# Modulation rows turned four at a time, and heads' products in two split passes, in a two-layer diffusion trunk on one core

## The reference

```
mod = silu(cond) @ w_ada + b_ada                 # (group, 6 * 1024)
h = rms_norm(x, norm1_g) * (1 + sc1) + sh1
z = h @ w_in                                     # 3,360 columns for mixers, 4,096 gate logits
aq, ak = rms_norm(a_q per head of 64), rms_norm(a_k per head of 64)
cq, ck = rms_norm(c_q per head of 32), rms_norm(c_k per head of 32)
aq, ak, cq, ck = apply_rope(...)                 # latent tokens only: y = x*cos + rot(x)*sin
...                                              # attention A and C, gated recurrences B and D
x = x + g1 * (sum(sigmoid(logits) * branches) @ w_out)
x = x + g2 * conv_ffn(rms_norm(x)*(1+sc2)+sh2)
```

## Time and profile before

| | |
|---|---|
| median of 3 runs | 2597.76 us (2597.54 to 2599.13) |
| profiled execution, its own time | 2600.3 us |
| span of the profiled execution | 2598.5 us |
| granted clock of TensorE, mean | 0.976 of full |
| busy: PE, PE weight loads, DVE, ACT | 95%, 89%, 52%, 35% |
| moved by DMA | 228.54 MB, 88 GB/s |

### The profile page before, as it was taken

One profiled execution on the slowest core, in us unless ns is written; L12 is line 12 of the kernel. 1 busy time (PEld: TensorE's weight loads), 2 busy tenths in 40 slices (PEclk: granted clock), 3 DMA queues, 4 the chain that ended last, 5 costly groups with the idle time before them and its releaser, 6 DMA issues.

```text
span 2598.5 us, 50531 instructions
## 1 busy us (share of the span) xinstructions
PE 2471.3 (95%) x22106; PEld 2303.3 (89%) x22106; DVE 1343.4 (52%) x2075; ACT 919.6 (35%) x1290; POOL 2.2 (0%) x6
## 2 busy tenths in 40 slices
PE   5999899899999999999989998979999999999998
PEld 3889776788999899999989996768899989999998
DVE  4123366786755655454241325768775654555621
ACT  4244355322243533333232435542222543333410
POOL 0000000000000000000000000000000000000000
PEclk8999899899999999999999998989999999999999
DMA  8645111122235222213244331102222622222222
GB/s 252 198 156 165 31 43 37 44 55 59 63 126 160 65 69 77 81 50 98 77 143 138 110 95 41 47 26 53 52 63 79 206 65 66 81 70 71 68 70 71
DMA packets 323607, 228.54 MB, mean 88 GB/s; under 512 B 17952, under 2 KB 317024, under 8 KB 322656
## 3 DMA queue, kind: packets, MB, share of 16 engines
q1 hardware_dynamic: 317584, 211.32, 27.8%
q10 hardware_dynamic: 5840, 14.51, 1.7%
HBM read 215.44 MB, written 10.35 MB: 87 GB/s over the span
## 4 chain that ended last, share of the span: by engine, by line
PE 83%; DVE 10%; ACT 3%; issue 2%; DMA 1%; SPq 0%; DVEq 0%; ACTq 0%
PE PS L681 21%; PE PS L682 21%; PE PS L683 21%; PE PS L883 2%; DVE RING_split L1740 2%; PE PS L850 2%; PE PS L898 1%; PE PS L705 1%; PE PS L914 1%; PE PS L670 1%; PE PS L993 1%; DVE BIG L1914 1%; PE PS L793 1%; PE PS L852 1%; PE PS L794 1%
## 5 line engine op out<-in xcount | busy, mean ns | idle before, releaser
L681 PE MATMUL PS<-HH_split,WHI_split 128*128 128x320 f32 x3168 | 999.8, 316 | 21.4 <-DVE HL_split L1715 8.6
L683 PE MATMUL PS<-HH_split,RING_split 128*128 128x320 f32 x3136 | 973.6, 310 | 0.0
L682 PE MATMUL PS<-HL_split,WHI_split 128*128 128x320 f32 x2912 | 905.9, 311 | 0.0
L681 PEld LDWEIGHTS PS<-HH_split,WHI_split 128*128 128x128 f32 x3168 | 600.1, 189 | 36.0 <-issue 25.2
L683 PEld LDWEIGHTS PS<-HH_split,RING_split 128*128 128x128 f32 x3136 | 593.2, 189 | 0.0
L682 PEld LDWEIGHTS PS<-HL_split,WHI_split 128*128 128x128 f32 x2912 | 552.5, 190 | 1.9 <-issue 1.9
L1740 DVE TENSOR_TENSOR RING_split<-RING,WHI_split 128x1024 fp32r<-128x1024 f32 (+2 forms) x204 | 274.6, 1348 | 473.0 <-ACT WHI_split L1473 235.2
L682 PE MATMUL PS<-ZT_split,WHI_split 128*128 128x320 f32 x1216 | 377.1, 310 | 0.0
L682 PEld LDWEIGHTS PS<-ZT_split,WHI_split 128*128 128x128 f32 x1216 | 229.5, 189 | 0.0
L1747 DVE TENSOR_TENSOR RING_split<-RING,WHI_split 128x1024 fp32r<-128x1024 f32 x52 | 62.4, 1223 | 263.0 <-ACT WHI_split L1215 262.9
L1473 ACT ACTIVATE WHI_split<-RING 128x1024 fp32r<-128x1024 f32 x88 | 93.3, 1060 | 289.6 <-PE PS L683 289.6
(11 more groups left out here) (215 smaller groups left out, 3293.6 us busy)
## 6 DMA issues: line engine op xcount, KB each, us to landing
RING<-in_w_in SPq DMA_DIRECT2D x96, 512.0 KB, 4.0
RING<-in_w_up SPq DMA_DIRECT2D x88, 512.0 KB, 5.0
RING<-in_w_ada SPq DMA_DIRECT2D x80, 512.0 KB, 6.1
RING<-in_w_down SPq DMA_DIRECT2D x32, 384.0 KB, 3.6
RING<-in_w_in SPq DMA_DIRECT2D x40, 256.0 KB, 3.3
RING<-in_w_down SPq DMA_DIRECT2D x32, 320.0 KB, 4.0
RING<-in_w_out SPq DMA_DIRECT2D x16, 512.0 KB, 4.7
ZT<-in_w_ada SPq DMA_DIRECT2D x8, 1024.0 KB, 10.0
```

Of the source, the lines that this page charges most:

```text
L681: release(pe.matmul(out, w_hi, hi[:, a:b], start=begin, stop=False), fresh and a == 0)
L682: pe.matmul(out, w_hi, lo[:, a:b], start=False, stop=False)
L683: ins = pe.matmul(out, w_lo, hi[:, a:b], start=False, stop=end)
```

## The change

Four things are changed.

1. After the first 8 modulation chunks, chunks go in sets of four (ADA_SET). The condition columns stand in SC32 with zeros on both sides, and a window on it places the two result rows of chunk r of a set at rows 2r and 2r + 1; the other rows get zeros, so the four products add up in one PSUM tile. Only the fourth is copied out, and one turn with 8 columns of SEL gives the set. The 8 chunks for layer 1 come in plain order so that sets are contiguous.
2. The heads' mean squares and the rotations are made in the split type: ACT rounds the operand (HI), DVE subtracts (LO), and PE makes two passes, HI and LO, against constants that are exact in the split type (copied once at the start by DVE).
3. Orders of issue: in layer 0's first tiles turn 4 comes before the products, modulation 6 and 7 one k apart, ACT's row copies before `modulate_two`, and DVE's weight rests before `modulation_first(1)`. ACT reads decay 0 (`decay_in(0)`) after the first tile of the last chunk.
4. `unit_order` looks two chunks ahead only after the second tile of chunk 3.

```diff
-        jobs = [(l, s) for s in range(N_ADA1, N_ADA_Z)] + ([(l + 1, s) for s in ADA1] if l + 1 < DEPTH else [])
+        jobs = [(l, s) for s in range(N_ADA1, N_ADA_Z)] + ([(l + 1, s) for s in range(N_ADA1)] if l + 1 < DEPTH else [])
...
+ADA_SET = 4
+def ada_row(a):
+    return 0 if a < N_ADA1 else (a - N_ADA1) % ADA_SET
+def ada_turns(a):
+    return a + 1 if a < N_ADA1 else N_ADA1 + (a - N_ADA1) // ADA_SET + 1
...
-            while nxt < U_MIX and nxt <= done + LEAD and chunk[nxt] <= c + (2 if c + 1 == QK_AT else 1):
+            while nxt < U_MIX and nxt <= done + LEAD and chunk[nxt] <= c + (2 if c + 1 == QK_AT and n == 1 else 1):
...
                 def ada_turn(a):
-                    pe.wait_ge(row_kept, a + 1)
+                    n = 1 if a < N_ADA1 else ADA_SET
+                    pe.wait_ge(row_kept, ada_turns(a))
                     for h in range(2):
-                        at = ada_at(a) + 2 * h
-                        last = pe.matmul(ada_columns(a)[:, at:at + 2], ROW[a % 2][:, h * P:(h + 1) * P], SEL[:], start=True, stop=True)
+                        out = ada_columns(a)[:, ada_at(a - n + 1):ada_at(a - n + 1) + 4 * n].rearrange("p (s h c) -> p s h c", h=2, c=2)[:, :, h, :]
+                        last = pe.matmul(out, ROW[ada_turns(a) % 2][:, h * P:(h + 1) * P], SEL[:, 0:2 * n], start=True, stop=True)
...
-                    if l == 0 and k == 1:
-                        first_turn(4)
                     if l == 0 and k == 2:
                         ada(5)
                         first_turn(5)
-                    if l == 0 and k == 4:
+                    if l == 0 and k == 3:
                         ada(6)
                         first_turn(6)
+                    if l == 0 and k == 4:
                         ada(7)
                         first_turn(7)
...
-                    wide(pair(2), BLK64 if QK_TILES[i][2] == 64 else BLK32, SQ[i % 2], True, True).then_inc(qk_ms, 1)
+                    pe.wait_ge(consts_split, 1)
+                    blocks = BLK64_R if QK_TILES[i][2] == 64 else BLK32_R
+                    wide(pair(2), blocks, SQ_HI[i % 2], True, False)
+                    wide(pair(2), blocks, SQ_LO[i % 2], False, True).then_inc(qk_ms, 1)
...
-                    pe.wait_ge(qk_normed, l * NQK + (i + 1))
-                    if i:
-                        pe.wait_ge(qk_done, l * NQK + i)
-                    pe.matmul(pair(3)[:, 0:TS], ROTA if hd == 64 else ROTC, ZT[:, t, 0:TS], start=True, stop=True).then_inc(qk_rot, 1)
+                    pe.wait_ge(rot_lo, l * NQK + (i + 1))
+                    turn_by = ROTA_R if hd == 64 else ROTC_R
+                    pe.matmul(pair(3)[:, 0:TS], turn_by, ROT_HI, start=True, stop=False)
+                    pe.matmul(pair(3)[:, 0:TS], turn_by, ROT_LO, start=False, stop=True).then_inc(qk_rot, 1)
...
+                        if n == 0 and 0 <= c - QK_AT - 2 < NQK:
+                            head_round(c - QK_AT - 2)
+                        if c == NC_Z - 1 and n == 0:
+                            decay_in(0)
...
+            nv.tensor_copy(CONST_R[:, 2 * P:], CONST[:, 2 * P:]).then_inc(consts_split, 1)
```

More of the change, by code:

```diff
@@ L704, in ada @@
                     for k in range(KT):
-                        last = pe.matmul(ada_out(a)[32 * (k % 4):32 * (k % 4) + 32], SC32[:, k, :], raw(RING, i, 0, 256, 256, KT)[:, k, :],
-                                         start=k < 4, stop=k >= 4)
+                        last = pe.matmul(ada_out(a)[32 * (k % 4):32 * (k % 4) + 32], SC32[:, k, SC_AT - 2 * ada_row(a):SC_AT - 2 * ada_row(a) + 32],
+                                         raw(RING, i, 0, 256, 256, KT)[:, k, :], start=k < 4 and ada_row(a) == 0,
+                                         stop=k >= 4 and (a < N_ADA1 or ada_row(a) == ADA_SET - 1))
                         release(last, k == 0, inside)
@@ L752, in _ @@
                             first_turn(a - 1)
+                    first_turn(4)
                 def head_mean_square(i):
@@ L1081, in late_turn @@
                         at = 4 * n + 2 * h
-                        last = pe.matmul(LATE_COLUMNS[:, at:at + 2], ROW[n % 2][:, h * P:(h + 1) * P], SEL[:], start=True, stop=True)
+                        last = pe.matmul(LATE_COLUMNS[:, at:at + 2], ROW[n % 2][:, h * P:(h + 1) * P], SEL[:, 0:2], start=True, stop=True)
                     last.then_inc(late_turned, 1)
@@ L1318, in _ @@
                 log_and_exp()
[L1319 to L1324 removed]
+                decay_in(1)
                 act.wait_ge(al_lin, l * 2 + 2)
@@ L1792, in _ @@
                 for c in range(NC_Z):
-                    for g, kind, dst, j in Z_TILES[c]:
+                    for n, (g, kind, dst, j) in enumerate(Z_TILES[c]):
                         for u in UNITS_AT[U_Z[g]]:
```

93 lines of the change are left out of this document (61 added, 32 removed).

## The result

| kernel | median of its runs, us | ratio to the kernel before, with 95% interval |
|---|---|---|
| before, 4 runs | 2598.45 (2597.54 to 2604.91) | |
| the change, 4 runs | 2566.88 (2563.29 to 2568.43) | 0.9862 [0.9851, 0.9874] |
| the same change again, later, 4 runs | 2565.58 (2564.58 to 2567.84) | 0.9864 [0.9849, 0.9879] |

The change is faster by 1.4%, or 31.6 us between the medians; 2567 was forecast. The profiled execution took 2566.3 us, 34.0 less than that of before. The forecast's terms, 30.7 us, are to be held against these 34.0 or against the 31.6 between the medians; the 2.5 us that it took off besides only led from the profiled execution of before to its median. The total is met closely, but by terms that were not: some were too small and some too large.

What follows compares the result with a forecast made beforehand. The prediction took PE to bound the kernel, busy in 95% of the span. Its terms summed to 30.7 us; 2600.3 less 30.7 and 2.5 (profiled run to median) gave 2567 us, range 2557 to 2579.

Steps and rivals of the forecast that it cites:

- What bounds the stage: Input-projection stage: a microsecond taken from PE is one of the kernel; ACT and DVE work is free if in time.
- Turns, 7.8: SEL products between PE's matmuls, both layers: 24 go, 23 counted here at 0.34 us each, 7.8 us gained.
- Mean squares, 3.2: 14 heads' mean squares: split passes cost 1.05 us instead of 1.28, 0.23 each, 3.2 us gained; bounds 2.4 and 6.9.
- rival 3: Short split products in the mean squares cost only their columns, 0.059 us: 4 us more gained, 2563 us; chance 0.15.
- Rotations, 4.4: 14 rotations as two split products: 0.39 us less each, 5.5, minus 1.1 lost waiting in layer 0's chunk 12.
- Start, 5.5: Start of layer 0: new orders end turn 7 sooner, less the constants' copy; 5.5 us net, bounds 4 to 8.
- Stop, 0.8: PE's stop at 127 us in layer 0: no turn there, still waits for chunk 5, ends at 132.9; 0.8 us gained.
- Ends, 9.0: Stage end, both layers: early decay 0 read lets PE go on, gates at half clock; 4.5 us each, bounds 8 and 14.
- 1 (layer 0 waits for weights): Faster PE in layer 0 waits for weight chunks from the four-slot ring, losing gains there: 2581 us; chance 0.12.
- 2 (the ends do not move): At the stage's ends decay 1 meets another wait, so the 9 us gain is lost: 2576 us; chance 0.08.
- 4 (PE waits at every rotation): PE waits at each rotation for ACT's rounding; 3.5 us each gives 2616 us, slower; chance 0.03.

Runs made afterwards that it cites:

- the kernel with the early weights sooner: The change with ACT's copy and DVE's rest of the early gate chunk moved behind the last chunk's first tile: 2560.1 us.
- both kernels with other mean squares: The change with the heads' mean squares in plain float32, 2570.81 us, and with each in ten split products of 128 columns, 2573.79 us.

## Why the prediction was right, and where not

- **What bounds the stage**: right. Busy time of PE taken from its body came out in the total; the added ACT and DVE work stayed hidden but for chunk 12.
- **Turns, 7.8**: right. 32 records of 2 columns and 32 of 8 remain, 8 turns each. All 24 undone cost 2.9 in layer 1 and 5.0 in layer 0 at equal clock, 7.9 together, and 8.4 in the total; the forecast counted 23 of them here and one with the stop.
- **Mean squares, 3.2**: mis-sized. The step that failed is "a load of 128x128 weights takes 0.19 us, which a short stream can hardly cover". A short piece costs 0.11, with what the next product loses, and 2 x (0.19 - 0.11) x 14 = 2.2 us are just what was missing: the term is 5.4 to 5.6 us, within its bounds of 2.4 and 6.9. This lies between the forecast and rival 3 (0.15), whose price of 0.059 is the distance to the next start alone. (The prediction's 0.54 us for a mean square leaves out the restart of 0.2, which its 4 us contain.)
- **Rotations, 4.4**: the mechanism and the price on PE were right (0.37 for 0.39), and so was the wait in chunk 12. What was left out is what an idle time does to the clock behind it. In the usual execution (nine traces of eleven) the term is 2.6 in layer 1 and close to nothing in layer 0, about 2.5 us; in the first trace, where the clock stayed full, it was about 4.0.
- **Start, 5.5**: 4.6 in the first trace and 5.9 in the second, but only in part by the cause that was given. The orders account for 3 to 4 us; 2.0 us are there without them, in the kernel with all orders back (its first modulation product behind chunk 0's first tiles begins at 65.16, before at 67.11), with the clock that came back at 43 us in place of 50. The order of turn 4 and the rests went as worked out; turn 7 began at 54.16 and 52.81, under the 55 that was asked for. Modulation 4 began at 33.4 to 34.7 us in the thirteen traces (33.41 before), and nothing shows that the constants' copy delays it.
- **Stop, 0.8**: the stretch to the V chunk is 3.2 us shorter (2.9 in the second trace), five turns of it 1.7. But behind it the clock was half for 3.4 or 6.8 us, and up to the next modulation product that takes back 0.6 or 1.6. What is left for the stop and the look ahead is 0.9 us in the first trace and -0.4 in the second, the usual one.
- **Ends, 9.0**: mis-sized. Measured 6.0 and 5.3, 11.3 together. The step that failed is the gates at half clock throughout (6.4 us): they ran at full clock for the first 1.4 us and the last 0.4, at half between, 5.2 us. It was known to be a choice between 4.0 and 7.0, and the result lay between. DVE as the engine that is late next was right, and the kernel with the early weights sooner shows what it costs.
- **Rivals**: 1 (layer 0 waits for weights) did not happen: layer 0 gained 20.4 us up to its scores. 2 (the ends do not move) did not either. 4 (PE waits at every rotation) happened once in fourteen.
- **The sum**. By the stretches of both traces and what the edits undone cost in them (us):

| term | forecast | first trace | second trace |
|---|---|---|---|
| turns (23) | 7.8 | 7.6 | 7.6 |
| mean squares | 3.2 | 5.4 | 5.4 |
| rotations | 4.4 | 4.0 | 2.5 |
| start | 5.5 | 4.6 | 5.9 |
| stop | 0.8 | 0.9 | -0.4 |
| ends | 9.0 | 11.3 | 11.3 |
| sum | 30.7 | 33.8 | 32.3 |
| measured, the stage and its edges | | 34.1 | 32.7 |
| measured, outside it (no edit there) | | 0.0 | 3.1 |

Mean squares and ends were 2.2 and 2.3 us too small, the rotations and the stop too large in the usual execution, and of the start 2 us came by a cause that was not forecast. Between the medians the gain is 31.6. The closeness of the total is in part luck; the range was not.

## What to carry to other kernels

The price of a short product is read from the distance between starts, of loads as well as of products, and the product behind it is read along with it; the duration of one weight load is no floor. An idle time of PE costs more than its length: what comes behind it may run at half clock, here for 3.4 us or for 6.8, so a wait of 1.6 us that is cut to 0.6 gave 2.5. When a chain over two engines is to be sooner, look at both queues: moving it up on one of them alone made PE wait longer here, 1.56 us in place of 1.05. That moving it on both would help is not shown.

## What the runs showed of the hardware that was not expected

- After idle times of the same length (1.05 us) at the same place, the clock stayed full in two traces and went to half for 3.4 us in nine. After the 0.5 to 0.6 us at the ends of the kernel with the early weights sooner it stayed full. After 1.61 in the first trace it fell 1.4 us behind the restart and came back 3.4 us later.
- The same idle time can also cost more or less: at the end of layer 1, behind 1.5 us, half clock held for 3.4 us in most traces and for 6.8 in three (the chunks turned one by one and both kernels with other mean squares), whose end took some 10 us in place of 8.9. No edit of theirs lengthens the idle time there; what decides it is open.
- This is one source of scatter: 1.5 us at one place, where a kernel's own runs spread by 2.5 to 8.6 us. Another lies where the change touches nothing: from the scores of layer 0 to layer 1 it took 1038.0 to 1040.0 us in most traces and 1042.3 and 1042.4 in two (the rests back, the look ahead back), and from the scores of layer 1 to the end 1019.9 to 1024.1. Single parts worth 1 to 3 us could be told only by stage, not by the total.
- Split products of 128 columns: 0.11 us each, in a row of ten as between long ones, where they show as 0.06 to the next start and 0.05 more on the product behind; loads of 0.19 overlap.
- A turn with 8 moving columns takes the same 0.34 us as with 2.
